# The end of a fused decoder layer: order of the last four weight units, place of GpSimd's test, no GpSimd drain, no last barrier

## The reference, cut to what matters

```python
for gi in range(N_EXPERT_GROUPS):
    hg = jnp.einsum('nd,edf->nef', x, p['w_gate'][gi])
    hu = jnp.einsum('nd,edf->nef', x, p['w_up'][gi])
    h = jax.nn.silu(hg) * hu * combine[:, gi, :, None]
    y = y + jnp.einsum('nef,efd->nd', h, p['w_down'][gi])
return y                                # layer output: h + y
```

## Time and profile before

| | |
|---|---|
| time, median of 3 runs | 1080.23 us |
| span of the profiled execution, first to last instruction | 1077.6 us |
| TensorE matmul busy | 913.1 us, 85% |
| VectorE, ScalarE, GpSimd busy | 324.4, 193.2, 112.9 us |
| last weight half lands | about 1060.4 us |
| last TensorE product ends | about 1065.7 us |
| GpSimd's drain at the end of the block | 4.05 us |

### The profile page before, as it was taken

One profiled execution on the slowest core, in us unless ns is written; L12 is line 12 of the kernel. 1 busy time (PEld: TensorE's weight loads), 2 busy tenths in 40 slices (PEclk: granted clock), 3 DMA queues, 4 the chain that ended last, 5 costly groups with the idle time before them and its releaser, 6 DMA issues.

```text
span 1077.6 us, 13517 instructions
## 1 busy us (share of the span) xinstructions
PE 913.1 (85%) x5419; PEld 496.5 (46%) x5419; DVE 324.4 (30%) x697; ACT 193.2 (18%) x462; POOL 112.9 (10%) x131
## 2 busy tenths in 40 slices
PE   3899969999967798799999899979887777787874
PEld 2455535555536454444556555535443334344441
DVE  3333242323244368864625111111110111111110
ACT  1111122112102456563100010000000000000000
POOL 0000114121000000000000012111110111110111
PEclk9999988999979768989998999999999999999998
DMA  9754017495405200003748999999999999999992
GB/s 387 319 174 125 15 55 182 109 222 121 134 1 183 102 1 1 1 1 149 296 184 319 360 415 417 408 417 418 407 419 416 416 413 410 409 419 414 412 418 72
DMA packets 66055, 273.14 MB, mean 253 GB/s; under 512 B 11760, under 2 KB 27951, under 8 KB 40575
## 3 DMA queue, kind: packets, MB, share of 16 engines
q1 hardware_dynamic: 52215, 255.22, 60.7%
q0 software_dynamic: 7376, 12.85, 4.4%
q10 hardware_dynamic: 6400, 4.20, 1.7%
HBM read 265.68 MB, written 19.10 MB: 264 GB/s over the span
## 4 chain that ended last, share of the span: by engine, by line
PE 27%; DMA 23%; SPq 8%; DVE 6%; ACT 3%; issue 1%; POOL 0%; DVEq 0%; POOLq 0%
DMA room<-in_w_up 13%; PE ps L2149 8%; SPq L2011 6%; PE ps L1721 5%; DMA w_a<-in_w_gate 5%; PE ps L2176 4%; DMA w_b<-in_w_up 3%; SPq L2015 2%; ACT w_a L1561 2%; DVE room L1426 2%; PE ps L1254 1%; PE ps L1272 1%; PE ps L1304 1%; PE ps L2163 1%; DMA xg<-hn_dram,pairs 1%
## 5 line engine op out<-in xcount | busy, mean ns | idle before, releaser
L2149 PE MATMUL ps<-room 128*64 128x256 f32 x800 | 98.1, 393 | 32.2 <-DMA room<-in_w_up 19.5
L2149 PEld LDWEIGHTS ps<-room 128*64 128x64 f32 x800 | 56.5, 140 | 70.2 <-DMA room<-in_w_up 28.7
L2149 PE MATMUL ps<-w_a,room 128*64 128x256 f32 x576 | 69.3, 390 | 17.2 <-DMA w_a<-in_w_up 9.3
L2149 PE MATMUL ps<-w_b,room 128*64 128x256 f32 x576 | 67.8, 383 | 17.8 <-DMA w_b<-in_w_up 9.5
L445 PE MATMUL ps<-w_b,room 128*128 128x454 f32 (+1 forms) x240 | 81.6, 551 | 0.7 <-ACT room L418 0.7
L2065 POOL DMA_INDIRECT out_y<-room,halves x32 | 50.1, 1566 | 286.4 <-ACT room L2329 286.4
L2329 ACT ACTIVATE room<-ps,slot_w 128x512 f32<-128x512 f32 x32 | 22.0, 687 | 281.0 <-PE ps L2176 281.0
L894 PE MATMUL ps<-room,w_a 128*128 128x378 f32 x192 | 62.0, 482 | 0.0
L2149 PEld LDWEIGHTS ps<-w_a,room 128*64 128x64 f32 x576 | 41.1, 139 | 42.7 <-DMA w_a<-in_w_up 13.9
L2149 PEld LDWEIGHTS ps<-w_b,room 128*64 128x64 f32 x576 | 40.2, 137 | 42.7 <-DMA w_b<-in_w_up 14.6
L2240 DVE SCALAR_TENSOR_TENSOR room<-room,ps 128x256 f32<-128x256 f32 x32 | 13.5, 422 | 152.6 <-ACT room L2323 152.6
(11 more groups left out here) (356 smaller groups left out, 1203.6 us busy)
## 6 DMA issues: line engine op xcount, KB each, us to landing
room<-in_w_down SPq DMA_DIRECT2D x26, 1024.0 KB, 28.8
room<-in_w_gate SPq DMA_DIRECT2D x25, 1024.0 KB, 28.4
room<-in_w_up SPq DMA_DIRECT2D x25, 1024.0 KB, 28.3
w_a<-in_w_gate SPq DMA_DIRECT2D x18, 1024.0 KB, 27.8
w_a<-in_w_up SPq DMA_DIRECT2D x18, 1024.0 KB, 28.5
w_a<-in_w_down SPq DMA_DIRECT2D x18, 1024.0 KB, 28.0
w_b<-in_w_gate SPq DMA_DIRECT2D x18, 1024.0 KB, 27.6
w_b<-in_w_up SPq DMA_DIRECT2D x18, 1024.0 KB, 28.3
```

Of the source, the lines that this page charges most:

```text
L2149: ins = nc.tensor.matmul(ps[h * CAP:h * CAP + CAP, bank, 0:FH], xT[:, n // 2 % 2, k, CAP * slot:CAP * slot + CAP], w[k // 4][:, k % 4, h * ...
```

## The change

Four edits, all at the end of the program. The last four units are asked for in the order 93, 94, 92, 95 (gate 31, up 31, down 30, down 31). GpSimd's wait for all scatters moves from ahead of its test to behind the block of the test (with a copy inside it). The second block ends without GpSimd's drain. The last `close` clears the semaphores and makes no barrier after that.

```diff
-    def close(self, stage):
+    def close(self, stage, last=False):
         stage.close()
         self.nc.clear_and_free_semaphores(self.stage_sems)
-        self.nc.all_engine_barrier()
+        if not last:
+            self.nc.all_engine_barrier()
         self.stage_sems = []
...
-        with self.nc.Block("attend_to_experts") as block:
+        with self.nc.Block("attend_to_experts", no_gpsimd_drain=True) as block:
...
-        self.close(st_e)
+        self.close(st_e, last=True)
...
             again = [3 * n + m + RING for n, m in uses[:24]]
-            again += [u for u in range(RING, NU) if u not in again]
+            again += [u for u in range(RING, NU - 4) if u not in again]
+            again += [NU - 3, NU - 2, NU - 4, NU - 1]
...
             pool.wait_ge(self.moved, 32)
-            pool.wait_ge(y_out, 16 * NEXP)
 
             with needed(pool):
+                pool.wait_ge(y_out, 16 * NEXP)
                 pool.wait_ge(x_turned, NEXP)
...
                     pool.wait_ge(o_y_out, 16 * (j + 1))
                     pool.sem_inc(tile_free, 1)
+            pool.wait_ge(y_out, 16 * NEXP)
```

## The result

| | before | after |
|---|---|---|
| time, median of 13 runs each | 1079.83 us | 1068.78 us |
| ratio of the times | | 0.9913, 95% interval 0.9889 to 0.9937 |
| span of the profiled execution | 1077.6 us | 1069.2 us |
| issue of the first of the last eight weight halves | 1015.2 us | 1015.7 us |
| from there to the end of the span ("the tail") | 62.4 us | 53.5 us |

The change makes the kernel 0.87% faster, 9.4 us by the ratio. The forecast was 8.9 us on the span and 1071.3 us in time. The tail, which the rest of this text measures with, became 8.9 us shorter.

What follows compares the result with a forecast made beforehand. Weight traffic bounds the experts, then a serial tail after the last weights. Gains 3.4 + 1.2 + 4.05 + 0.3 = 8.9 us put the span at 1068.7; with 2.6 us around it, 1071.3 us, range 1069.9 to 1076.0.

Steps and rivals of the forecast that it cites:

- The order: Last four weight units: landings keep their times and change owners, down 31 ends at 1062.3 instead of 1065.70; gain 3.4 us.
- Scatter 30: Second to last scatter: starts at 1058.9, flies 3.9 us, lands at 1062.8, just ahead of ScalarE's end at 1063.0.
- The bound of 8.4 us: Flight of a scatter beside full weight traffic; with it scatter 30 would land at 1067.3.
- rival (c): Scatter 30 becomes the bound: with 8.4 us of flight, scatter 31 lands 4.3 us late; 1075.6 us, chance 0.04.
- The test: GpSimd's load of the count, decoding and branch run under scatter 31's flight; 1.2 of 1.4 us gained.
- rival (b): Block's end: part returns, through an uncovered instruction fetch or 1.0 us kept by the next drain; 1072.4 us, chance 0.10.
- The drain: GpSimd's drain at the second block's end: 4.05 us taken as gained, with the clearing's drain staying at 0.2 us.
- rival (a): The drain's work moves on: the clearing's drain or whatever empties GpSimd later takes the 4.05 us; 1075.4 us, chance 0.27.
- The last barrier: Barrier behind the last clearing: without it the span ends with the clearing; gain 0.3 us, bound above 1.0 us.
- the 2.6 us around the span: Distance of the profiled span 1077.6 from the median time 1080.23, taken as unchanged and added to the predicted span.
- Rival (d): New order brings nothing, halves late or TensorE slower when dense: 1074.7 us with the drain gone, else 1078.7; chance 0.05.
- rival (e): Slower: the end outside the span grows because what follows must wait for GpSimd; for instance 1083 us, chance 0.04.

## Why the prediction was right

**The order: 3.4 us predicted, 3.2 us alone, 3.3 us in the whole.** The landings kept their times and changed owners, as the step had it. (A slip in its reading, without effect on the landings: the second half of the last pair is issued 1.6 us behind the first, not 2.1 to 2.6.) On the clock of before down 30 ended at 1057.5 (predicted 1057.4), down 31 at 1062.4 (1062.3), scatter 31 started at 1063.9 (1063.8). A small error inside is swallowed. I took 1.95 us for each group of 16 products; without pauses between them two groups take 3.6 to 3.7 us, and the rows overlap. TensorE is therefore 0.8 us earlier at down 30 than I had it (1053.0 against 1053.75), and there waits 0.72 us for the second half, where I had the products and the landing meet. The landing was the bound in either case.

**Scatter 30: 3.9 us taken, 3.7 to 3.8 us measured.** The bound of 8.4 us and with it rival (c) are out: with one half in flight, and that for its first 1.4 us only, the scatter flew as without traffic. It landed 0.4 us ahead of the end of ScalarE's row (1063.3 against 1063.67).

**The test: 1.2 us predicted, 1.2 us alone.** The cover was larger than I had it. I let the load of the count begin when the scatter's row ends; it began before that row (1064.2 against 1064.4). The jump out of the block took 0.2 us, as assumed, so rival (b) is out too: one fetch still shows in the last 4 us (at 1066.2), but it lies beneath the wait, and the next drain kept no 1.0 us.

**The drain: 4.05 us predicted, 3.8 us alone, 4.3 us between the whole and all but the drain.** The size is right and the reason only half so. I chose the reading in which the long and the short drain are different things, and called the other one (bookkeeping for the DMAs made before, done by the next drain) rival (a) with 0.27. The runs show that the bookkeeping is real and that the next plain drain does pay for it; what saves the change is that the clearing comes first, and that it strikes the debt without paying. The row I had for it, 203 ns, stood behind a full drain and couldn't tell. The first block could have: its drain had 1.0 us over its fill, which I put down as a remainder in rival (b) because no indirect DMA ran there, and it is the debt of 11 plain ones. That the work "has to be done by someone" was true of plain drains and not of the clearing. So the gain hung on a property of the clearing that no row before showed; with the chance at 0.50 that step came out right by luck as much as by reasoning. With a plain drain ahead of the clearing the change would have gained 4 us less.

**The last barrier: 0.3 us predicted.** The run with it alone shows 0.1 us, with 0.2 us lost to a slower scatter; behind the landing of scatter 31 it shows the 0.3 us.

**The time itself: 1071.3 us predicted, 1068.78 us measured.** The span of the profiled execution after is 1069.2 us, 1068.7 on the clock of before, which is the number predicted. One term was off, the 2.6 us around the span: I took them as the distance of one execution's span from the median of others. Every execution recorded since has both, and they are 2.1 us apart. The remaining 2 us lie in the spans: the median execution after has a span of 1066.7 us, 2.5 us under the profiled one. The profiles differ in when they reach the last units and hardly in the tail, so I put the 2 us there; no trace of the median execution shows it. It is chance and no merit of the sum, and it is what takes the median out of the range. The ratio, 9.4 us, compares best with the 8.9 us of the sum.

Rival (d), the order without effect, and rival (e), a longer end outside the span, are refuted by the run with the order alone and by the 2.1 us.

## What to carry to other kernels

Ask for the last transfers in the order in which they are used: behind a queue that is always full the landings keep their times, and a landing that is needed two steps later than its place on the queue holds up everything behind it. GpSimd's plain drain had a price here for each DMA that it had issued since its last plain drain, so look at its row at the end of each block. Waiting on the count of the last DMA took its place here only because the clearing came next; where a plain drain comes next, that one pays. The other way is to drain earlier, where the engine has slack. And when the executions scatter by 1%, measure an edit at the end of a program from a fixed event near it to the end of the span.

## What the runs showed of the hardware that I had not expected

- GpSimd's plain drain took 3.99 to 4.05 us with 48 of its DMAs since the last one, 3.89 us with 47, 1.76 us with 20, 0.20 us with one, 40 ns right behind another: some 82 ns for each. With a gather in flight it took 5.6 us with 28, where the line gives 2.4 us, and ended 1.2 us after the gather's landing.
- The drain at the head of the semaphore clearing took 190 ns with the whole debt open, and the plain drain behind it 54 ns.
- A load of a register from SBUF on GpSimd's sequencer began 0.2 us before the row of the indirect DMA that stands ahead of it in the program (1064.2 against 1064.4).
- The sixth of the last eight halves comes late in every order: in the run with the order alone the products behind it wait 0.71 us, after it is 0.72 us, and before it was the second half of up 31, issued 2.16 us behind the first and landing 3.0 us behind it. Scatter 29 is in flight then; whether it is what makes that half late was not tried.
